# Shifted copies of a convolution chunk by way of DRAM, a gate moved ahead of two splits, and a later clearing

## The reference, cut to what matters

```python
def conv_mixer(x, past, w_in, b_in, w_dw, b_dw, g_ln, b_ln, w_out):
    h = x @ w_in + b_in
    u = h[..., :D_CONV] * jax.nn.sigmoid(h[..., D_CONV:])
    if past is None:
        buf = jnp.pad(u, ((0, 0), (CONV_WIDTH - 1, 0), (0, 0)))
    else:
        buf = jnp.concatenate([past.astype(u.dtype), u], axis=1)
    conv = lax.conv_general_dilated(buf, w_dw[:, None, :].astype(u.dtype), window_strides=(1,), padding='VALID',
                                    dimension_numbers=('NWC', 'WIO', 'NWC'), feature_group_count=D_CONV) + b_dw
    y = jax.nn.silu(layer_norm(conv, g_ln, b_ln)) @ w_out
    return y, buf[:, -(CONV_WIDTH - 1):, :]
```

## Time and profile before

| | us |
|---|---|
| median of 3 runs | 1722.65 |
| the profiled execution's own time | 1724.23 |
| its span, first to last instruction | 1722.6 |
| TensorE busy (matmul) | 1605.6 (93%) |
| VectorE busy | 998.8 (58%) |
| ScalarE busy | 750.4 (44%) |
| GpSimd busy | 147.4 (9%) |

### The profile page before, as it was taken

One profiled execution on the slowest core, in us unless ns is written; L12 is line 12 of the kernel. 1 busy time (PEld: TensorE's weight loads), 2 busy tenths in 40 slices (PEclk: granted clock), 3 DMA queues, 4 the chain that ended last, 5 costly groups with the idle time before them and its releaser, 6 DMA issues.

```text
span 1722.6 us, 27537 instructions
## 1 busy us (share of the span) xinstructions
PE 1605.6 (93%) x10670; PEld 1218.0 (71%) x10670; DVE 998.8 (58%) x1233; ACT 750.4 (44%) x829; POOL 147.4 (9%) x267
## 2 busy tenths in 40 slices
PE   8879999999998999999898989787899999999897
PEld 6758899998965666855344526454688888888685
DVE  4568755447636554573213313231688888888797
ACT  3225543225434223242212312221677777777575
POOL 1350000000031541020000000000000000000300
PEclk9989999999989999989999999888999999999999
DMA  8759454443240541059999999999999999999992
GB/s 237 204 160 312 123 163 148 135 144 115 98 138 23 150 125 42 2 189 363 403 401 404 404 406 396 404 403 388 410 408 371 395 378 364 399 367 370 392 366 112
DMA packets 235517, 465.61 MB, mean 270 GB/s; under 512 B 26613, under 2 KB 125204, under 8 KB 235393
## 3 DMA queue, kind: packets, MB, share of 16 engines
q1 hardware_dynamic: 217438, 426.96, 68.0%
q0 software_dynamic: 11744, 27.78, 5.0%
q10 hardware_dynamic: 6227, 9.40, 1.7%
HBM read 440.86 MB, written 18.76 MB: 267 GB/s over the span
## 4 chain that ended last, share of the span: by engine, by line
PE 72%; DMA 9%; DVE 7%; ACT 5%; ACTq 3%; issue 2%; SPq 1%; POOL 0%; POOLq 0%; DVEq 0%
PE ps L2677 10%; PE ps L2833 8%; PE ps L2834 8%; PE ps L2835 8%; PE ps L2136 6%; PE ps L2138 6%; PE ps L2137 6%; DMA raw<-in_moe_w_gu 5%; PE ps L2670 3%; ACTq L777 2%; PE ps L2671 2%; PE ps L2672 2%; DMA raw<-in_moe_w_down 2%; PE ps L2519 2%; PE ps L2482 2%
## 5 line engine op out<-in xcount | busy, mean ns | idle before, releaser
L1987 DVE TENSOR_TENSOR w_lo<-raw,w_hi 128x2048 fp32r<-128x2048 f32 x168 | 383.2, 2291 | 59.9 <-ACT w_hi L1294 58.9
L1294 ACT ACTIVATE w_hi<-raw 128x2048 fp32r<-128x2048 f32 x168 | 322.3, 1919 | 132.4 <-PE ps L2835 114.6
L1993 DVE TENSOR_TENSOR w_lo<-raw,w_hi 128x2048 fp32r<-128x2048 f32 x42 | 96.3, 2292 | 229.6 <-ACT w_hi L1301 229.6
L2136 PE MATMUL ps<-x_hi,w_hi 128*128 128x304 f32 x672 | 207.8, 309 | 3.1 <-DVE x_lo L1539 1.6
L2138 PE MATMUL ps<-x_lo,w_hi 128*128 128x304 f32 x672 | 202.8, 302 | 0.0
L2137 PE MATMUL ps<-x_hi,w_lo 128*128 128x304 f32 x672 | 202.0, 301 | 0.0
L1429 DVE TENSOR_TENSOR w_lo<-raw,w_hi 128x2048 fp32r<-128x2048 f32 (+4 forms) x129 | 135.6, 1098 | 96.4 <-ACT w_hi L1039 96.3
L2833 PE MATMUL ps<-w_hi,g_hi 128*128 128x512 f32 x448 | 177.5, 396 | 12.6 <-DVE w_lo L1987 12.6
L1039 ACT ACTIVATE w_hi<-raw 128x2048 fp32r<-128x2048 f32 (+4 forms) x129 | 115.5, 949 | 142.0 <-PE ps L2138 65.9
L2835 PE MATMUL ps<-w_hi,g_lo 128*128 128x512 f32 x448 | 175.7, 392 | 0.0
L2834 PE MATMUL ps<-w_lo,g_hi 128*128 128x512 f32 x448 | 175.6, 392 | 0.0
(11 more groups left out here) (464 smaller groups left out, 2507.2 us busy)
## 6 DMA issues: line engine op xcount, KB each, us to landing
raw<-in_moe_w_gu SPq DMA_DIRECT2D x224, 1024.0 KB, 9.8
raw<-in_moe_w_down SPq DMA_DIRECT2D x112, 1024.0 KB, 10.0
raw<-in_ffn_w_gu SPq DMA_DIRECT2D x44, 512.0 KB, 5.1
raw<-in_conv_w_in SPq DMA_DIRECT2D x16, 512.0 KB, 9.5
raw<-in_ffn_w_down SPq DMA_DIRECT2D x16, 512.0 KB, 4.0
kvn<-in_cache_ckv POOLq DMA_DIRECT2D x64, 128.0 KB, 3.4
kvn<-in_cache_ckv SPq DMA_DIRECT2D x64, 128.0 KB, 2.6
rows_in<-zrow POOLq DMA_DIRECT2D x13, 512.0 KB, 13.0
```

The source lines that it names most:

```text
L1294: nc.scalar.activation(w_hi[:, u % SPLIT], raw[:, u % RAW], ACT.Copy).then_inc(hi_done, 1)
L1987: V.tensor_tensor(w_lo[:, u % SPLIT], raw[:, u % RAW], w_hi[:, u % SPLIT].bitcast(F32), ALU.subtract).then_inc(lo_done, 1)
L1993: V.tensor_tensor(w_lo[:, n % F_SPLIT], first_raw(k), w_hi[:, n % F_SPLIT].bitcast(F32), ALU.subtract).then_inc(lo_done, 1)
L2136: nc.tensor.matmul(out, hi, xh, start=start, stop=False, skip_group_check=True)
```

## The change

Three edits. First, the shifted copies of a chunk are made by GpSimd alone and in two steps: one store of the whole chunk, 128 x 302 numbers, into a new DRAM table `u_rows`, then a wait until it has landed, then four loads, one for each shift, that read the table with the four groups side by side. ScalarE and SyncE issue no copies any more, and one semaphore counts the four loads. Second, for chunk 7 the gate on ScalarE and the multiplication on VectorE stand ahead of the split of unit 9, not behind it. Third, GpSimd's stores of zeros wait until taps 7 are done.

```diff
+    u_rows = nc.dram_tensor("u_rows", [DC, P, U4_READ], F32, kind="Internal").ap()
...
-    def shift_rows(engine, m, shifts, ready):
+    def shift_rows(engine, m):
 
         engine.wait_ge(group_free, m + 1)
+        engine.dma_start(u_rows[m], u_p[:, m, :]).then_inc(u_out, 16)
         if m >= 2:
             engine.wait_ge(tap_w_used, m - 1)
-        for s in shifts:
-            for g in range(SHIFTS):
-                n = min(U4, U4_READ - s)
-                engine.dma_start(u4[m % 2][GROUP * s:GROUP * s + GROUP, g, 0:n], u_p[GROUP * g:GROUP * g + GROUP, m, s:s + n]
-                                 ).then_inc(ready[m % 2], 16)
+        engine.wait_ge(u_out, 16 * (m + 1))
+        for s in range(SHIFTS):
+            n = min(U4, U4_READ - s)
+            engine.dma_start(u4[m % 2][GROUP * s:GROUP * s + GROUP, :, 0:n],
+                             u_rows[m, :, s:s + n].rearrange("(g c) n -> c g n", g=SHIFTS)).then_inc(u4_ready[m % 2], 16)
...
         for u in range(2, U_GU):
             load(u)
-        shift_rows(sp, DC - 1, (0,), u4_ready)
...
         for m in range(DC):
-            shift_rows(pool, m, (2, 3) if m < DC - 1 else (2,), u4_more)
+            shift_rows(pool, m)
...
         pool.wait_ge(zrow_made, 1)
+        pool.wait_ge(tap_w_used, DC)
...
         for m in range(8):
-            split(U_CIN + m + AHEAD)
+            if m < DC - 1:
+                split(U_CIN + m + AHEAD)
             act.wait_ge(unit_used, U_CIN + m + 1)
             if m >= 2:
                 act.wait_ge(group_free, m - 1)
             nc.scalar.activation(gate[:, m % 2], ps[:, group_bank(G_CIN + m) + 1, 0:T], ACT.Sigmoid,
                                  bias=b_in[:, DC + m:DC + m + 1]).then_inc(gate_ready, 1)
-            shift_rows(act, m, (0, 1) if m < DC - 1 else (1, 3), u4_ready)
+            if m == DC - 1:
+                split(U_CIN + m + AHEAD)
...
         for m in range(8):
-            split(U_CIN + m + AHEAD)
+            if m < DC - 1:
+                split(U_CIN + m + AHEAD)
             v.wait_ge(gate_ready, m + 1)
...
             v.wait_ge(group_free, m + 1)
+            if m == DC - 1:
+                split(U_CIN + m + AHEAD)
             if m >= 2:
                 add_taps(m - 2)
...
-            last_part = SHIFTS if m == DC - 1 else 0
-            pe.wait_ge(u4_ready[m % 2], 16 * (2 * SHIFTS * (m // 2 + 1) + last_part))
-            pe.wait_ge(u4_more[m % 2], 16 * (2 * SHIFTS * (m // 2 + 1) - last_part))
+            pe.wait_ge(u4_ready[m % 2], 16 * SHIFTS * (m // 2 + 1))
```

More of the change, by code:

```diff
@@ L503, in build @@
     u4_ready = [sem(f"u4_ready{b}") for b in range(2)]
-    u4_more = [sem(f"u4_more{b}") for b in range(2)]
+    u_out = sem("u_out")
     tap_w_ready = sem("tap_w_ready")
```

## The result

Five runs of the changed kernel gave a median of 1730.9 us (1725.7 to 1732.34), five of the kernel before beside them 1722.24 us. The ratio with its 95% interval is 1.0037 [1.0022, 1.0051], so the change makes the kernel slower by a little that is clear of the noise, where 1716.9 us was forecast. (Ratios here are the recorded estimates over all runs; the quotient of the two medians is 1.0050.) The profiled execution took 1732.34 us (span 1730.7), 8.1 us more than the one before (1724.23, span 1722.6). The page's totals tell little: TensorE is busy for 1609.0 us, VectorE for 998.1, as before. The time is in waits at three places, and each stands in one timeline.

A forecast was written before the change was run, and what follows sets the result against it. TensorE's waits for copies before taps 0 (5.04 us) and taps 7 (9.69 us) were taken as the bound. Gain 8.7 at the end less X 2.9 plus 0 for clearing is 5.8: 1722.65 to 1716.9 us, range 1713.5 to 1721.5.

The forecast's parts named there:

- Part 1: Start of the convolution block: store and loads of chunk 0 start taps 0 at 52.0 instead of 49.46, costing 2.9 us.
- X: Delay of the whole 64.7 us TensorE block that starts with taps 0, forecast at +2.9 us including 0.4 for the clock.
- the same block: TensorE's stretch from taps 0 to 114.1 keeps its 64.7 us length and only moves as a whole.
- The rival of X from 5.3 up: Block start: X of 5.3 to 8.7 eats the gain, 1719.2 to 1722.6 us, say 1720.5; chance 0.18.
- A flight of over 9 us: Chunk 0: store or loads take over 9 us each, taps 0 past 58.2, slower than before, 1724; chance 0.06.
- X near zero: Block start: both flights of chunk 0 take 4 to 4.5 us, no delay, 1714.0 us; chance 0.12.
- Part 2: Mixer's end: chunk 7's copies start 3.1 us earlier, land at 116.5 beside one weight load; variance 8.7 us earlier before X.
- Up to 4 us of further lateness of the copies would therefore be hidden: Chunk 7: VectorE's own chain ends after taps 7, so copies up to 4 us later would cost nothing.
- The rival in which VectorE starves the descriptors: GpSimd's DMAs each wait out a VectorE instruction of up to 2.29 us, X about 14, 1728 or more; chance 0.02.
- Part 3: Zeros stored after taps 7: cost 0, bounded by 1 us if they slow some load of the next product.
- the same 1586 us: Sign: the time from the variance (line 1526) to the end stays 1586 us; a change over 1 us means wrong.
- My chance of 0.08 for slower: Together, the over-9 us flights of chunk 0 (0.06) and VectorE holding up descriptors (0.02) make the kernel slower.

The follow-up runs named there:

- zeros last: Changed kernel with GpSimd's stores of zeros waiting for the landing of the edge stores instead of for taps 7; 1723.79 us, ratio 1.0006.
- weights held: Changed kernel with SyncE's loads of the dense weights held until taps 7 are done; 1726.75 us, ratio 1.0017.
- two mends: Changed kernel with dense weights held until taps 7 are done and zeros stored behind the edge stores' landing, chunk 0 still by DRAM; 1717.63 us, ratio 0.9968.
- zeros early: Changed kernel without the third edit, so GpSimd's stores of zeros do not wait for taps 7; 1725.18 us, ratio 1.0006.
- the repeat: The changed kernel itself, run again unaltered as the base line for the variants; 1732.35 us, ratio 1.0044 against the kernel before.
- chunk 0's direct copies: Changed kernel with chunk 0's 16 copies made straight from u_p, 8 from each queue, as before; 1731.05 us, ratio 1.0044.

## Why the prediction was wrong

**Part 1, nearly right.** "Taps 0 at 52.0" was 52.45, and within the 51 to 54 that I had named. The sum behind it had the store at 5.8 (measured 5.06) and the load at 6.5 (8.03), so two misses of opposite sign cancel in part. Its reason for low figures, that ScalarE's half of the copy traffic is gone, does not hold for the loads: four of 150 KB carry what sixteen of 37 KB did, and the store comes on top. The clock was priced at 0.4 us and cost 1.0 (6.57 - 5.56): X was 4.0, not 2.9. "From there the same block" held. The rival of X from 5.3 up did not occur in the two traces of the changed kernel (4.0 and 4.6), but the kernel with the zeros last, which is the same up to there, had 5.5. A flight of over 9 us or an X near zero did not occur in any.

**Part 2, a mis-sized term.** The failed step is "One weight load of the dense layer falls beside them, as unit 15 follows the split that ends at 111.4; 1 to 2 us more, so 116.5." I had the right load at the right moment and half its size: the unit is two issues of 512 KB, 1 MB. The last load flew 7.46 us, where I had 2.6 and up to 2 more, and with the weights held it flew 3.4. The allowance for lateness ("Up to 4 us of further lateness of the copies would therefore be hidden") was then used up: taps 7 came 5.1 us behind the forecast and ran at half clock, 2.5 us longer. The first mean, the squares and VectorE's chain were as I had them, as the kernel with weights held shows: from the end of the row of 128 (118.83) to its variance (132.33) are 13.5 us, where I had 127.7 - 114.1 = 13.6. The changed kernel with two mends, in which neither weights nor zeros fly beside chunk 7, comes nearest to the forecast's case: with its X of 4.0 the forecast's 127.7 becomes 131.7, and 131.64 was measured.

One step of this part was wrong without showing in the sum. It lets the second edit bring the copies of chunk 7 forward by 3.1 us. In the changed kernel that edit brings u_p forward by nothing: u_p starts 0.66 us behind the start of the row of 128 with the edit (111.24 against 110.58) and without it (111.08 against 110.42). Freed of its issues by the first edit, ScalarE waits for the product of chunk 7 either way, 10.69 or 8.89 us. What the order does move is VectorE, whose first mean stands 8.89 us behind that row with the edit and 5.50 without.

The rival in which VectorE starves the descriptors is out. With the weights held the loads from GpSimd's queue landed in 3.1 to 3.4 us, in a stretch where VectorE was busy in 3.93 of 4 us. The Trainium skill (page "SBUF — State Buffer", section "SBUF: two separate sides") has such a stall for VectorE's two-port modes; the trace shows none with these instructions.

By the Trainium skill (page "DMA: Bandwidth & Descriptors", section "Anatomy of one DMA") 150 KB from GpSimd's queue would take some 2.35 us, an estimate from its 2.0 us plus the bytes at 436 GB/s. The quiet flights here (2.5 to 2.9 for the store, 3.1 to 3.4 for the loads) lie a little over it, the loaded ones, 5.06 to 8.03, at two to three and a half times of it.

**Part 3, a missed consequence, and the largest.** The failed step is "Cost 0, bounded by 1 us if the stores slow some load of the next product." I had asked who waits for the zeros' semaphore and which weights are still to be loaded. I had not asked which DMAs other engines issue in the new stretch, and what computation stands behind these issues on the same queue. ScalarE's eight edge stores need 3.53 us before and 10.77 after, and its next split is behind them. Two edits show it from both sides: zeros early or zeros last remove it (-7.2 and -8.6 us in the median), and zeros behind taps 7 in the kernel before bring it back (10.98). The prediction's own sign says the same: from the variance to the end it wanted "the same 1586 us", and it was 1593.2.

**The sum.** I had +2.9 - 8.7 + 0 = -5.8; it is +4.0 - 2.9 + 7.0 = +8.1. The middle term lost 5.8 us, and holding the weights gives as much back at the variance (138.15 against 132.33); the last was put at nothing. Without the third term it would have been +1.1, no difference that can be measured; the kernel with the zeros early has 1.0006. My chance of 0.08 for slower was tied to chunk 0's flights alone. What fell on the slower side was another mechanism, for which I had no rival.

**What stays open.** Single executions drift apart by some us at the start of the expert stage: by the starts of ScalarE's table loads the repeat was 10.3 us behind the kernel before at 494 us, 11.2 at 749, 7.3 at 786 and 8.0 at 1686. That may be why chunk 0's direct copies, worth 2.4 to 4.1 us at taps 2 and the variance, showed nothing in the median; it is not shown. Why the expert stage gives back or takes such amounts I did not try. Why the small stores are slow to issue stays open too. The engines' share alone is not it: it is 1.01 over the 10.8 us of the changed kernel and 1.06 over the 2.7 us of the one with two mends. The zeros beside them are the condition; by what way they act, no run tells.

## What to carry to other kernels

When a bulk transfer is moved out of one stretch, read every engine's queue in the stretch that it lands in, and for each small DMA there ask what computation of that engine stands behind its issue; a list of waiters on the transfer's own semaphore leaves these out. Take the size of a competing load from the issues' row (count times KB), and place it behind the latency-bound copies by a wait, which here was worth 5.6 us. A round trip through DRAM is two exposed flights in a row, and either of them can meet a burst: here the unit of weights met the loads in one order of the splits and the store in the other.

## What the runs showed of the hardware

- **An issue on ScalarE's queue has no fixed price.** A store of edge rows costs 0.34 us (2.73 for 8) with no zeros beside it, 0.44 (3.53) in the kernel before, 1.35 (10.77) while 512 KB stores of zeros from GpSimd's queue are under way. The DMA engines' share over these stretches is 1.06 (the kernel with two mends), 0.87 and 1.01, so a full set of engines alone does not slow the issue.
- **GpSimd's queue can stand still with no open wait in the program.** In the zeros-early kernel the first zeros follow four issued loads only after 6.69 us that the timeline puts to "issue", although their one wait (for the zeroed row, made in the first microseconds) had long been met. The last of those loads landed at 124.32, 0.4 us after the first zeros were issued. Behind the four direct copies of 37 KB in the kernel before there was no such pause (113.26). One case, and no cause shown.
- **Two levels of the clock at taps 7.** Behind waits of 2.04, 2.39, 2.45, 2.60, 2.63 and 2.90 us the taps took 3.87 us; behind those of 3.03 us and more they took 5.17 to 6.54. In the two kernels that differ only in how chunk 7's copies are divided, a start 0.52 us later (116.65 against 116.13) came with 1.69 us more for the taps.
